# A decoder layer in one launch: wider key rounds, an earlier page table and a third row buffer

## What is computed

```python
def hybrid_layer(x, p, attend, conv_buf, C0, n0, m0, lam_init, w):
    h = rmsnorm(x, w['pre_g'])
    u = h @ w['w_in']                                   # 1024 x 3584
    qa, ka, va, za, xb, ob, zb = jnp.split(u, SPLITS, axis=-1)
    a = attend(q, k, v, lam)                            # 4 heads, two softmax maps each
    a = headwise_rmsnorm(a, w['attn_g']) * (1.0 - lam_init)
    a = a.reshape(B, S, D_A) * jax.nn.silu(za)
    xc, new_buf = causal_conv(xb, conv_buf, w['conv_w'], w['conv_b'])
    ...
    hb, C1, n1, m1 = mlstm_scan(qb, kb, vb, ig, lf, C0, n0, m0)
    hb = headwise_rmsnorm(hb * sigmoid(ob), w['mlstm_g']) + w['mlstm_skip'] * xch
    y = jnp.concatenate([a, hb * jax.nn.silu(zb)], axis=-1) @ w['w_out']
    x = x + rmsnorm(y, w['post_g'])
    gate = jax.nn.sigmoid(x @ w['ple_gate'])
    return x + rmsnorm(gate * (p @ w['ple_w']), w['ple_g']), ...

def diff_attend(q, k, v, q_pos, k_pos, lam):
    s = einsum('bqhmd,bkhmd->bhmqk', q, k) * DK_A ** -0.5
    p = softmax(where(k_pos <= q_pos, s, -inf))
    w = p[:, :, 0] - lam * p[:, :, 1]
    return einsum('bhqk,bkhd->bqhd', w, v)
```

## Time and profile before

| | |
|---|---|
| median of three runs | 1026.84 us |
| the profiled execution | 1028.52 us, of which the span (first to last instruction) is 1026.9 |
| TensorE busy, granted clock | 919.8 us, mean 0.955 of 2.4 GHz |
| VectorE, ScalarE, GpSimd busy | 519.4, 356.5, 143.5 us |
| moved by DMA | 142.74 MB, mean 139 GB/s |
| scores of keys, batch 0 and batch 1 | 2048 records each, 301.3 to 386.3 and 545.8 to 643.8 us |

### The profile page before, as it was taken

The page is one execution under the profiler, slowest core; times in us unless marked ns, Lnnn a source line. Parts: engine busy times, 40 slices in busy tenths (PEclk is TensorE's granted clock), DMA queues, the critical chain, the costliest instruction groups (busy, mean ns, idle before and its releaser), DMA issues. The chain is left out here.

```text
span 1026.9 us, 24358 instructions
## 1 busy us (share of the span) xinstructions
PE 919.8 (90%) x10051; PEld 733.2 (71%) x10051; DVE 519.4 (51%) x1066; ACT 356.5 (35%) x777; POOL 143.5 (14%) x306
## 2 busy tenths in 40 slices
PE   4999999999869899999986878787999999999996
PEld 3989889999747676887764645555667787677774
DVE  4633845455358444455547757454567443343122
ACT  5444353334211142533344212434564322422111
POOL 2300000000312100000031112222341000000000
PEclk9999999999969999999998888899998999999998
DMA  7352215222467642222148565486894622113221
GB/s 231 83 164 63 83 42 144 63 63 63 141 203 238 210 155 63 62 82 63 41 147 291 173 161 199 146 267 242 297 391 144 247 82 85 62 33 113 79 102 41
DMA packets 111833, 142.74 MB, mean 139 GB/s; under 512 B 9751, under 2 KB 75927, under 8 KB 111722
## 3 DMA queue, kind: packets, MB, share of 16 engines
q1 hardware_dynamic: 101482, 107.62, 33.2%
q0 software_dynamic: 10240, 33.56, 9.4%
HBM read 125.34 MB, written 15.41 MB: 137 GB/s over the span
## 5 line engine op out<-in xcount | busy, mean ns | idle before, releaser
L2083 PE MATMUL ps<-hhi,whi 128*128 128x272 f32 (+1 forms) x672 | 234.0, 348 | 4.5 <-DVE wlo L1412 2.5
L2083 PE MATMUL ps<-hhi,wlo 128*128 128x272 f32 (+1 forms) x672 | 222.0, 330 | 0.0
L2083 PE MATMUL ps<-hlo,whi 128*128 128x272 f32 (+1 forms) x672 | 221.8, 330 | 0.0
L2083 PE MATMUL ps<-wh,r 128*128 128x512 f32 (+1 forms) x544 | 154.3, 399 | 0.4 <-DVE wout_lo L1963 0.3
L2083 PEld LDWEIGHTS ps<-hhi,whi 128*128 128x128 f32 x672 | 130.5, 194 | 21.0 <-issue 8.7
L2083 PEld LDWEIGHTS ps<-hlo,whi 128*128 128x128 f32 x672 | 130.6, 194 | 11.1 <-issue 3.2
L2083 PEld LDWEIGHTS ps<-hhi,wlo 128*128 128x128 f32 x672 | 130.4, 194 | 10.1
L1412 DVE TENSOR_TENSOR wlo<-wst,whi 128x1024 fp32r<-128x1024 f32 x56 | 68.8, 1229 | 125.1 <-ACT whi L999 125.1
L2083 PEld LDWEIGHTS ps<-wh,r 128*128 128x128 f32 (+1 forms) x544 | 98.5, 184 | 26.8 <-issue 1.6
L792 POOL TENSOR_TENSOR small<-small 128x1 f32<-128x1 f32 (+2 forms) x37 | 8.0, 215 | 483.4 <-ACT junk L1331 198.2
L2083 PE MATMUL ps<-U 64*128 64x512 f32 (+3 forms) x192 | 47.5, 574 | 22.0 <-DVE pp L1897 20.5
(11 more groups left out here) (367 smaller groups left out, 1427.6 us busy)
## 6 DMA issues: line engine op xcount, KB each, us to landing
wst<-in_w_in SPq DMA_DIRECT2D x56, 512.0 KB, 3.7
window_keys<-in_cache_k SPq DMA_DIRECT2D x32, 256.0 KB, 3.0
window_keys<-in_cache_k POOLq DMA_DIRECT2D x32, 256.0 KB, 5.2
Kr<-in_cache_k SPq DMA_DIRECT2D x32, 256.0 KB, 3.7
Kr<-in_cache_k POOLq DMA_DIRECT2D x32, 256.0 KB, 4.3
Vr<-in_cache_v SPq DMA_DIRECT2D x32, 256.0 KB, 4.0
Vr<-in_cache_v POOLq DMA_DIRECT2D x32, 256.0 KB, 4.7
Kr<-in_cache_v SPq DMA_DIRECT2D x32, 256.0 KB, 4.6
```

The costliest lines, as they stand in the source:

```text
L2083: return nc.tensor.matmul(out, lhsT, rhs, start=start, stop=stop, **more)
```

## The change

- A round is four pairs (`ROUND` = 4): 32 x 256 keys in each of the 64 matmuls, 8 rounds for a batch; two pieces go behind each round of the window. The ring stays 8 pairs, now two rounds deep, so pages of round g+2 may be loaded when round g has been scored. Each queue sends its two pairs of a round together. Convolutions 1 to 3 move to rounds 0 to 2.
- The page table is read early into `first_ptab` (at the end of the second half of U) and copied inside SBUF to `ptab` later; both queues load their first registers from `first_ptab`.
- GpSimd makes `q_new` right after the sample part is done, and clears `qk[0]` before it waits for chunk 3. `new_scores` waits for the `q_new` scalings only. The three clearings for chunk 4 move behind the first two rounds' pages.
- SP asks for weight tile 31 before the first key pages; tiles 32 and 33 stay behind the pages of the ring, and then one tile follows each round.
- In the attention `pp` becomes three buffers for units 0 to 23 (the third in the place of VA's second half) and two from there on. `head_rows` waits for the turns of unit u-3 instead of u-2. The output weights are loaded in another order, since two of them share the third buffer's place.
- `KEY_SHARE` goes from 0.36 to 0.33, and the steps at which value pages are asked for follow the new rounds.

```diff
-PER_ROUND = 1
+PER_ROUND = 2
...
+THIRD = 24
...
-ROUND = GROUPS // 4
+ROUND = GROUPS // 2
...
-VALUE_WAIT = (0, 0, ROUNDS - 3, ROUNDS - 3, ROUNDS - 2, ROUNDS - 2, ROUNDS, ROUNDS)
-VALUE_ISSUE = [max(LAST_KEYS, round_step(VALUE_WAIT[q] - 1)) + 1 + q % 2 if q < RING else VALUE_STEP[q - RING] + 1
+VALUE_WAIT = (0, 0, ROUNDS - 1, ROUNDS - 1, ROUNDS - 1, ROUNDS - 1, ROUNDS, ROUNDS)
+VALUE_ISSUE = [max(LAST_KEYS, round_step(VALUE_WAIT[q] - 1)) + 1 + (q - 2) % 4 if q < RING else VALUE_STEP[q - RING] + 1
...
-KEY_SHARE = 0.36
+KEY_SHARE = 0.33
...
-WOUT_AT = {15: 2, 17: 3, 19: 4, 21: 5, 23: 6, 25: 7, 27: 0, 28: 1}
-assert DECODED[CH + PHASES * 15] > KEY_STEPS + 1 and DECODED[CH + PHASES * 27] > TURN_STEP[0, 3] + 1
+WOUT_AT = {15: 4, 17: 5, 19: 6, 21: 7, 23: 0, 25: 1, 27: 2, 28: 3}
...
-        q_new = place("q_new", [P, BATCHES, H, 32], offset=u1_end - 1056)
+        first_ptab = place("first_ptab", [1, 2 * GP * KEY_STEPS], I32, offset=u1_end - 1056)
+        q_new = place("q_new", [P, BATCHES, H, 32], offset=u1_end - 1056 - 2080)
         q_rep = [place("q_rep0", [P, H, H, SMP // 2], offset=u1_end - 1056 - 2 * 2080),
                  place("q_rep1", [P, H, H, SMP // 2], offset=after_qbT1)]
         xb_new = place("xb_new", [P, H, SMP], offset=after_qbT1 + 1024)
         assert S1_new >= after_qbT1 + 1024 + 512
         qk = [place("qk0", [P, PACK, H, H, 32], offset=u0_base + OB * FIRST * 4),
               place("qk1", [P, PACK, H, H, 32], offset=rest_of_tail + GROUPS * 512 * 2)]
-        pp = place("pp", [P, 2, 2, SEQ], offset=u1_base + XB * HALF * 4)
+        pp_buffers = [place(f"pp{n}", [P, 2, SEQ], offset=u1_base + at * HALF * 4) for n, at in enumerate((XB, OB, VA))]
+
+        def pp(u):
+
+            return pp_buffers[u % 3 if u < THIRD else u % 2]
+
+        def turned_before(u):
+
+            return PARTS_BEFORE[u - 2 if u < THIRD + 2 else u - 1]
+
...
+            for turn in range(2):
+                first = KEY_STEPS * turn
+                sp.dma_start(first_ptab[0:1, first:first + KEY_STEPS].rearrange("o (b g k) -> o b g k", b=NSEQ, k=GP),
+                             io["page_table"][:, :].rearrange("(o b) (g q k) -> o q b g k", o=1, q=2, k=GP)[:, turn, :, :, :]
...
+            sp.wait_ge(s["ptab_in"], PTAB_IN)
+            sp.dma_start(ptab[0:1, :], first_ptab[0:1, :]).then_inc(s["ptab_in"], 16)
...
-                turn = n // ROUND
-                if turn % 4 == 0:
+                turn = n // 2
+                if turn % 4 == 0 and turn:
                     own_pages(GP * turn)
-                if n >= RING:
+                if n >= RING and n // ROUND - RING_ROUNDS + 1 > IN_ROUNDS * (n >= IN_BATCH):
                     sp.wait_ge(s["scores_ready"], n // ROUND - RING_ROUNDS + 1)
                 for k in range(GP):
...
-            sp.wait_ge(s["ptab_in"], PTAB_IN)
+            def round_pages(g):
+                for n in range(ROUND * g, ROUND * g + ROUND, 2):
+                    key_pages(n)
+
+            own_pages(0, first_ptab)
+            load_w(NT + 3)
             sp.wait_ge(s["bo_done"], H)
             sp.wait_ge(s["wqkv_in"], 64 + 64)
-            for g in range(RING_ROUNDS):
-                key_pages(ROUND * g)
-            for w in range(NT + 3, NT + 6):
-                load_w(w)
-            for g in range(RING_ROUNDS, IN_ROUNDS):
-                key_pages(ROUND * g)
-                if g % 2:
-                    load_w(NT + 4 + g // 2)
-            for w in range(NT + 4 + IN_ROUNDS // 2, WEIGHTS):
+            round_pages(0)
+            round_pages(1)
+            load_w(NT + 4)
+            load_w(NT + 5)
+            sp.wait_ge(s["ptab_in"], PTAB_IN + 16)
+            for g in range(2, IN_ROUNDS):
+                round_pages(g)
+                load_w(NT + 4 + g)
+            for w in range(NT + 4 + IN_ROUNDS, WEIGHTS):
                 load_w(w)
 
             def value_pages(q):
...
-                    if order < 2:
+                    if k in (2, 3):
+                        sp.wait_ge(s["wT_ready"], PARTS_BEFORE[THIRD])
+                    if k < 2:
                         sp.wait_ge(s["pT_ready"], turned(0, 3))
...
-                pool.wait_ge(s["zero_ready"], 16 + 4 + b)
+                pool.wait_ge(s["zero_ready"], 16 + (1, 5)[b])
...
-            pool.wait_ge(s["piece_done"], 2 * NT)
-            for z in (Ablk_[1], G_[1], vaug_[1]):
-                nc.gpsimd.memset(z[:], 1.0 if z is vaug_[1] else 0.0).then_inc(s["zero_ready"], 1)
-            pool.wait_ge(s["bo_done"], H)
-            pool.wait_ge(s["wqkv_in"], 64 + 64)
-            for g in range(RING_ROUNDS):
-                key_pages(ROUND * g + 1)
-            nc.gpsimd.memset(qk[0][:], 0.0).then_inc(s["zero_ready"], 1)
-            pool.wait_ge(*done["q_rep_stored"])
-            own_queries(0)
+            def round_pages(g):
+                for n in range(ROUND * g + 1, ROUND * g + ROUND, 2):
+                    key_pages(n)
+
+            pool.wait_ge(s["ptab_in"], PTAB_IN)
+            own_pages(KEY_STEPS, first_ptab)
+            pool.wait_ge(*done["s_bo"])
             new_q = tok(slice(QA, QA + H), SEQ, SMP).rearrange("p h (b j t) -> p b j h t", b=BATCHES, t=STEPS)
             for m in range(2):
                 for j in range(PACK):
                     own = q_new[:, :, :, 8 * j + 4 * m:8 * j + 4 * m + 4]
                     nc.gpsimd.tensor_scalar(own, new_q[:, :, j, :, :], map_scale[:, m:m + 1], 0.0, ALU.mult, ALU.add
                                             ).then_inc(s["q8_ready"], 1)
-            for g in range(RING_ROUNDS, IN_ROUNDS):
-                key_pages(ROUND * g + 1)
+            pool.wait_ge(s["obT_ready"], H)
+            nc.gpsimd.memset(qk[0][:], 0.0).then_inc(s["zero_ready"], 1)
+            pool.wait_ge(s["bo_done"], H)
+            pool.wait_ge(s["wqkv_in"], 64 + 64)
+            round_pages(0)
+            pool.wait_ge(*done["q_rep_stored"])
+            own_queries(0)
+            round_pages(1)
+            pool.wait_ge(s["piece_done"], 2 * NT)
+            for z in (Ablk_[1], G_[1], vaug_[1]):
+                nc.gpsimd.memset(z[:], 1.0 if z is vaug_[1] else 0.0).then_inc(s["zero_ready"], 1)
+            pool.wait_ge(s["ptab_in"], PTAB_IN + 16)
+            for g in range(2, IN_ROUNDS):
+                round_pages(g)
...
                     act.wait_ge(*done["new_scored"])
+                    act.wait_ge(s["ptab_in"], PTAB_IN + 16)
+                    act.wait_ge(s["scores_ready"], 1)
...
-                if g % 2 and g // 2 + 1 < H:
-                    conv_second(g // 2 + 1)
+                if g + 1 < H:
+                    conv_second(g + 1)
...
-                if u >= 2 and c == 0:
-                    dve.wait_ge(s["wT_ready"], PARTS_BEFORE[u - 1])
+                if u >= 3 and c == 0:
+                    dve.wait_ge(s["wT_ready"], turned_before(u))
...
-                        nc.vector.tensor_scalar(pp[:, u % 2, m, first:first + k], score_part(m, k), -QSCALE, -LOWEST,
+                        nc.vector.tensor_scalar(pp(u)[:, m, first:first + k], score_part(m, k), -QSCALE, -LOWEST,
...
-                pe.wait_ge(s["q8_ready"], NSEQ + 4 * PACK)
+                pe.wait_ge(s["q8_ready"], NSEQ + 2 * PACK)
...
-                    pe.wait_ge(s["q8_ready"], NSEQ + 2 * PACK * (1, 3)[b])
+                    pe.wait_ge(s["q8_ready"], NSEQ + 2 * PACK * (2, 3)[b])
```

More of the change, by code:

```diff
@@ L865, in _, with own_pages @@
             page = [None] * RING
-            def own_pages(first):
+            def own_pages(first, table=ptab):
                 page[:] = nc.values_load_multi_w_load_instructions(
-                    ptab[0:1, first:first + RING], engines=[mybir.EngineType.Pool], min_val=0, max_val=POOL - 1)[1]
+                    table[0:1, first:first + RING], engines=[mybir.EngineType.Pool], min_val=0, max_val=POOL - 1)[1]
             def key_pages(n):
-                turn = n // ROUND
-                if turn % 4 == 0:
+                turn = n // 2
+                if turn % 4 == 0 and turn:
                     own_pages(KEY_STEPS + GP * turn)
-                if n >= RING:
+                if n >= RING and n // ROUND - RING_ROUNDS + 1 > IN_ROUNDS * (n >= IN_BATCH):
                     pool.wait_ge(s["scores_ready"], n // ROUND - RING_ROUNDS + 1)
@@ L2475, in head_turn @@
                 for q in range(k // P):
-                    last = turn(ps[:, 6, q * P:(q + 1) * P], pp[:, u % 2, 0, first + q * P:first + (q + 1) * P])
+                    last = turn(ps[:, 6, q * P:(q + 1) * P], pp(u)[:, 0, first + q * P:first + (q + 1) * P])
                 last.then_inc(s["wT_ready"], 1)
```

49 lines of the change are left out of this document (23 added, 26 removed).

## The result

The changed kernel takes 996.35 us in the median (993.75 to 1000.56) beside 1027.2 for the kernel before on the same chip: a ratio of 0.971 (0.965 to 0.976), 31 us less. The forecast was 982 in a range of 961 to 1007. The profiled execution took 997.51 us, its span is 995.9.

What follows compares the result with a forecast made beforehand. TensorE bounds the kernel, busy 919.8 of 1026.9 us. Window stage -18.5, key stretch -18.5 and value stretch -8 sum to -45, taking the profiled 1028.52 to 983.5, median about 982; range 961 to 1007.

Steps and rivals of the forecast that it cites:

- Start, -6.0: Start of the window: first key round at 295.3 us where it had started at 301.3, so -6.0.
- part 1: Before the first key round: queries and page table early; waits of 6.3 us (q_new) and 2.5 (tile 31) go.
- Wide rounds in the window, -11.7: Window: a wide round costs 2.4 us, its period 8.1 against 9.56 for two narrow ones; eight times 1.46 saved.
- Rival A: Rounds: width costs in proportion, sixteen wide rounds at 3.66 us instead of 2.4, +20, giving 1002; chance 0.08.
- Gaps, -3.3 and -5.2: TensorE's gaps with no releaser halve with half the instructions: -3.3 of 6.6 us in the window, -5.2 of 10.3 under attention.
- VectorE in the window, +1: Window's first three rounds: VectorE needs 9.1 us against a period of 8.1; TensorE meets at most a microsecond, +1.
- Key stretch, -18.5: Attention with batch 1's rounds: rounds -10.7, gaps -5.2, waits for rows -4.6, VectorE +3, clock -1; sum -18.5 us.
- the term "+3": Key stretch: VectorE, at 88% in a stretch 20 us shorter, will sometimes come last, costing 3 us.
- part 2: Window, rounds of four pairs: 12.2 us left for a page transfer of about 2 + 6.9, called enough.
- part 3: Batch 1's rounds under attention: 15 narrow and seven wide, 27.5 us becomes 16.8, -10.7; gaps halve, -5.2.
- Rival D: Two-round ring: VectorE waits for pages, weights and rows queue behind, TensorE stops; landings of 18 us give +70, 1052; chance 0.03.
- Rows in three buffers, -4.6 and -7: Attention: a third row buffer cuts TensorE's waits to about 0.5 us each, -4.6 in the key stretch, -7 in the value stretch.

Runs made afterwards that it cites:

- The four corners: Kernels with narrow or wide rounds and two or three row buffers; attention: narrow and two 245.3 us, narrow and three 232.3, wide and two 239.6, wide and three 232.3.
- e2: The kernel before with only the attention rows in three buffers and the new order of the last weights; 1012.99 us, ratio 0.987.

## Why the prediction came out as it did

**Start, -6.0: right by its mark, less so in its reasons.** Measured -5.7, and the chain was named (pages at 271, tile 32, VectorE's order, turns); the pages left at 274, in a profile whose mark is 2.5 later. The 6.3 us of q_new that part 1 speaks of were no part of it: with the queries late again nothing is lost. What gave the 5.7 is then the rest of part 1, the early table and the order of the queues, which no run takes apart. The sum was safe because the step had said of these waits "That doesn't give 8.8".

**Wide rounds in the window, -11.7 with 2.4 each: right in kind, 2.2 too much.** A round is 2.68 from its start to the next matmul, the period 8.38, eight times 1.18 is 9.5. Rival A (3.66) falls. By the Trainium skill, "TensorE: Matmul & The Clock Gate", section "Back-to-back issue gap", the distance between isolated matmuls grows as the columns. Twice the columns cost 1.46 times here (2.68 to 1.83). The prediction's reading that these tiles "don't follow that floor" of some 25 ns goes by records, 14.3 ns each (20.9 in the wide rounds). One issued matmul leaves two records, and from one issued matmul to the next it is 28.6 ns (41.9), above the page's figure. So nothing here contradicts the floor.

**Gaps, -3.3 and -5.2: too little.** They went from 16.8 in eleven to 2.7 in two, 5.7 in the window and 8.4 in the key stretch. With half the instructions more than half of the gaps went. The width changed with the number, and what makes the gaps no run shows.

**VectorE in the window, +1: nothing in the rounds.** But a wait that no step named came behind them, 2.6 us at chunk 4. The edit that takes it away gained 6.8 in the median and 4.7 in the mean of the lengths. It comes from two pieces after the last round where there had been one. I had written that the four chunks behind were unchanged. Their work was, their first wait wasn't.

**Key stretch, -18.5: this is the step that failed.** Measured -11.4. Its rounds came out as forecast, -10.8 (36.1 to 25.3) for -10.7, in part by luck: at the 2.68 measured at full clock, where 2.4 was taken, seven wide rounds for fifteen narrow ones give only -8.7, and the narrow ones of before cost 2.3 each instead of 1.83, several of them at the low clock. What failed is the term "+3" (VectorE "will sometimes come last"), and under it the 12.2 us of slack worked out for part 2 and then not worked out again for part 3. In the window a page has two periods, in the attention it has the steps between score and turn, five before and three after. VectorE waited 13.7 us for pages, and TensorE 15.8 for rows' first passes where the terms had left 4.0 (8.6 less 4.6) and +3. (Six waits of 0.5 would leave 3.0, so the step's own figures give -5.6, and in the value stretch -7.9; both terms were put smaller.) TensorE's idle time in the stretch should have fallen by 6.8 (-5.2, -4.6, +3) and rose by 2.5 (28.0 to 30.6). The clock, put at -1, went from 0.85 to 0.83.

Rival D had the mechanism, VectorE behind the pages with the rows behind it, but priced it by landings of 18 us in the window. In the attention they take 12.1 at the most. Long landings had a part, 2.96 of the 8.5 us drawn out above, but for most of the waits the turn only had to be early. One step more of distance gave 6.2 back. The four corners suggest for the rest that the row buffers' and the rounds' gains meet in the same waits; which instruction holds each is not shown.

**Rows in three buffers, -4.6 and -7: right.** Alone 13.0 for 11.6; beside the wide rounds 7.3. In the value stretch each wait is 0.5, as forecast. That stretch was -1.6 and not -8 because TensorE's waits fell by 5.2 and not 7, and because it is busy for 3.4 us more there. The latter fits KEY_SHARE 0.33, which moves row work from the key stretch into it and which no step costed; no run takes it alone. It flatters the key stretch by as much.

**The range.** Of the 45 us forecast 31 came. The 14 that are missing lie nearly all in the attention, 13.0 of 26.5. The time of 996.35 lies in the range all the same. That is partly luck: the upper end was made of a dearer round, gaps that stay, a late start and VectorE. What used most of it up was a wait for the ring in the attention, a mechanism that the prediction gave 0.03, and its size happened to fit.

## What to carry to other kernels

Count the slack of a ring in the order that its consumer keeps, as steps between the release of a slot and the use of what is loaded into it, for every stage in which the ring runs. Bigger units in the same ring shorten that distance even where the bandwidth suffices. And where a unit of a stage is doubled, look at what stands behind the last one: the wait at the seam belongs to no step of the stage and is easily left out of the sum.

## What the runs showed of the hardware

- In 32 x 32 tiles of fp32 a round of 128 records (64 issued matmuls) takes 1.83 us with 128 columns and 2.68 with 256 at full clock. At a granted clock of 0.52 the round of 256 took 4.36, and at 0.51 the one of 128 took 2.70: 1.6 and 1.5 times their time at full clock, not twice.
- TensorE's gaps without a releaser: with narrow rounds 16.8 us in eleven and, in e2, 20.2 in thirteen; with wide rounds, half as many matmuls and each twice as wide, 0.3 to 2.8 in one to four, in all twelve kernels.
- A single wait of 2.6 us between dense work at full clock lay ahead of 20 us with a mean granted clock of 0.84 to 0.91, in eight kernels; in the four without the wait it was 1.00 twice and 0.91 twice. After one and the same wait of 2.49 us the first round ran at full clock in one kernel and at 0.58 in another.
- Key pages of 256 KB for batch 1 took 5.7 us from issue to landing in the median and up to 12.1 in SyncE's queue; where VectorE waited for them longest (587 to 591) the transfers ran at 369 GB/s. Before, with four pages asked for at once instead of eight, the medians in the two queues were 3.7 and 4.3 us; after, 5.7 and 6.2.
